# Both heads' attention scores multiplied back to back behind the tenth chunk, with a second probability buffer

## The reference

```python
scores = jnp.einsum('brhnqd,brhnkd->brhnqk', qb, kc) * (dh ** -0.5)
scores = jnp.where(mask, scores, -jnp.inf)
m = scores.max(-1, keepdims=True)
pr = jnp.exp(scores - m)
denom = pr.sum(-1, keepdims=True)
out = jnp.einsum('brhnqk,brhnkd->brhnqd', pr, vc) / denom
...
inner = jnp.einsum('bhqk,bhkv->bhqv', jnp.einsum('bhqd,bhkd->bhqk', qc, kc) * intra_decay, vc)
...
ret = head_group_norm(ret, ret_gn_g, ret_gn_b)
ret = (jax.nn.silu(ret_g.astype(jnp.float32)) * ret).astype(x.dtype)
merged = jax.nn.sigmoid(gate_a) * (attn @ w_attn_proj) + jax.nn.sigmoid(gate_r) * (ret @ w_ret_proj)
return merged @ w_out
```

## Time and profile before

| | |
|---|---|
| median of three runs | 1491.69 us (1491.23 to 1495.32) |
| the profiled execution | 1495.06 us, span 1493.3 us |
| TensorE busy with matmuls | 1460.3 us, 98% of the span |
| VectorE busy | 1047.4 us, 70% |
| ScalarE busy | 768.7 us, 51% |
| GpSimd busy | 45.9 us, 3% |
| mean granted TensorE clock | 0.993 |
| DMA | 292.00 MB, mean 196 GB/s |

### The profile page before, as it was taken

The page is one execution under the profiler, slowest core; times in us unless marked ns, Lnnn a source line. Parts: engine busy times, 40 slices in busy tenths (PEclk is TensorE's granted clock), DMA queues, the critical chain, the costliest instruction groups (busy, mean ns, idle before and its releaser), DMA issues.

```text
span 1493.3 us, 20079 instructions
## 1 busy us (share of the span) xinstructions
PE 1460.3 (98%) x8177; PEld 1278.8 (86%) x8177; DVE 1047.4 (70%) x1189; ACT 768.7 (51%) x813; POOL 45.9 (3%) x30
## 2 busy tenths in 40 slices
PE   9999999999999999999999999999999999999998
PEld 8888888888888888888888888888887888888886
DVE  5775675857665588777857667667567556887777
ACT  5545454454554456566544454545545444566562
POOL 0000000000000020000000000000000000200000
PEclk9999999999999999999999999999999999999999
DMA  9777596685856564655555956857748664665571
GB/s 309 237 189 207 172 212 202 182 214 169 224 178 224 179 219 166 211 197 198 178 174 170 226 182 176 218 182 198 211 159 208 201 222 162 220 205 189 172 239 39
DMA packets 357420, 292.00 MB, mean 196 GB/s; under 512 B 104544, under 2 KB 347744, under 8 KB 356704
## 3 DMA queue, kind: packets, MB, share of 16 engines
q1 hardware_dynamic: 356528, 290.14, 64.4%
q10 hardware_dynamic: 816, 0.79, 0.2%
HBM read 277.27 MB, written 13.63 MB: 195 GB/s over the span
## 4 chain that ended last, share of the span: by engine, by line
PE 80%; DVE 11%; ACT 3%; DMA 3%; SPq 1%; issue 1%; DVEq 0%; ACTq 0%
PE bank L1394 34%; PE bank L1399 17%; PE bank L1380 6%; PE bank L1381 6%; PE bank L1382 6%; DVE w_lo L819 5%; PE acc L1380 3%; PE acc L1381 3%; PE acc L1382 3%; ACT w_hi L462 2%; DMA raw<-w_in 1%; SPq L316 1%; PE acc L1529 1%; DVE scratch L1030 1%; DVE stat L1015 1%
## 5 line engine op out<-in xcount | busy, mean ns | idle before, releaser
L819 DVE TENSOR_TENSOR w_lo<-raw,w_hi 128x2048 fp32r<-128x2048 f32 x234 | 535.4, 2289 | 201.7 <-ACT w_hi L462 201.3
L1394 PE MATMUL bank<-xT_both,w_hi 128*128 128x512 f32 x2208 | 528.4, 392 | 2.2 <-DVE scratch L976 2.2
L462 ACT ACTIVATE w_hi<-raw 128x2048 fp32r<-128x2048 f32 x241 | 459.3, 1908 | 118.6 <-PE bank L1382 50.8
L1394 PEld LDWEIGHTS bank<-xT_both,w_hi 128*128 128x128 f32 x2208 | 407.7, 188 | 83.5 <-DVE scratch L976 2.8
L1399 PEld LDWEIGHTS bank<-xT_both,w_lo 128*128 128x128 f32 x2208 | 283.1, 191 | 10.7
L1399 PE MATMUL bank<-xT_both,w_lo 128*128 128x256 f32 x2208 | 286.5, 283 | 0.0
L1380 PE MATMUL bank<-w_hi,xT_both 128*128 128x512 f32 (+1 forms) x464 | 164.2, 354 | 16.3 <-DVE w_lo L819 15.9
L1381 PE MATMUL bank<-w_lo,xT_both 128*128 128x512 f32 (+1 forms) x464 | 163.2, 352 | 0.0
L1382 PE MATMUL bank<-w_hi,xT_both 128*128 128x512 f32 (+1 forms) x464 | 162.8, 351 | 0.0
L573 ACT ACTIVATE scratch<-bank 128x512 f32<-128x512 f32 x80 | 47.6, 595 | 212.0 <-PE bank L1399 212.0
L1380 PEld LDWEIGHTS bank<-w_hi,xT_both 128*128 128x128 f32 x464 | 89.7, 193 | 29.2 <-issue 17.8
(11 more groups left out here) (170 smaller groups left out, 1351.7 us busy)
## 6 DMA issues: line engine op xcount, KB each, us to landing
raw<-w_in SPq DMA_DIRECT2D x133, 1024.0 KB, 5.1
raw<-w_up SPq DMA_DIRECT2D x44, 1024.0 KB, 5.1
raw<-w_down SPq DMA_DIRECT2D x20, 1024.0 KB, 5.1
raw<-w_ret_proj SPq DMA_DIRECT2D x16, 1024.0 KB, 5.4
prob_blocks<-scratch SPq DMA_DIRECT2D x16, 512.0 KB, 4.3
scratch<-prob_blocks SPq DMA_DIRECT2D x64, 128.0 KB, 4.2
raw<-w_attn_proj SPq DMA_DIRECT2D x8, 1024.0 KB, 5.3
raw<-w_out SPq DMA_DIRECT2D x8, 1024.0 KB, 5.2
```

Of the source, the lines that this page charges most:

```text
L462: nc.scalar.activation(w_hi[:, s, :], raw[:, s, :], ACT.Copy).then_inc(hi_ready, 1)
L819: nc.vector.tensor_tensor(w_lo[:, s, :], raw[:, s, :], w_hi[:, s, :].bitcast(F32), ALU.subtract).then_inc(lo_ready, 1)
L1394: mm(pair[p][:, m, :], hi[:, o:o + P], src[:, k0 + k, :, :].rearrange("p a t -> p (a t)"), start=first and k == 0, stop=False)
```

## The change

There are two probability buffers and two sets of row statistics. The second buffer lies where the rotary step's temporaries are before and where `ret_t` is after. Behind chunk 9 TensorE multiplies the scores of both heads, head 1 into `acc[2]` and `acc[3]`. VectorE masks head 1 right after the rotary step of chunk 10, and at c = 11 takes its maximum and then normalises and turns both heads. ScalarE takes head 1's exponential at c = 11. Behind load 1' SyncE issues both `prob_out`, behind 2' both `prob_in`, and behind 4' only retention's blocks. The number of instructions is the same.

```diff
-        prob = view(2048, (TT, 512))
+        prob = [view(2048, (TT, 512)), view(6912, (TT, 512))]
...
                 if c == 1:
                     prob_out(0, it)
+                    prob_out(1, it)
                 if c == 2:
                     prob_in(0, it)
+                    prob_in(1, it)
                 if c == 4:
-                    prob_out(1, it)
                     ret_out(it)
-                    prob_in(1, it)
                     ret_in(it)
...
-                    if c == 14:
-                        exp(1)
...
+                    if c == 11:
+                        exp(1)
...
-                def mask_and_max(a):
+                def mask_scores(a):
                     if a == 0:
                         dve.wait_ge(const_in, 16)
+                    else:
+                        dve.wait_ge(roped_ready, it2 + 2)
                     dve.wait_ge(scores_done, it2 + a + 1)
                     for t in range(TT):
-                        ins = nc.vector.tensor_tensor(prob[:, t, :], acc[t][:, :], mask[:, t, :], ALU.add)
+                        ins = nc.vector.tensor_tensor(prob[a][:, t, :], acc[2 * a + t][:, :], mask[:, t, :], ALU.add)
                     ins.then_inc(scores_masked, 1)
+
+                def scores_max(a):
...
                 def turn_ret():
 
                     dve.wait_ge(ret_y_ready, it + 1)
+                    dve.wait_ge(prob_turned, it2 + 2)
...
                     if c == 14:
                         high_part(13, silu[:, 0:2, :], 1.0)
-                        mask_and_max(1)
                         group_stats()
...
                     if c == 10:
-                        mask_and_max(0)
+                        mask_scores(0)
+                        scores_max(0)
                         rotate(1)
+                        mask_scores(1)
                     if c == 11:
-                        normalise(0)
-                        turn_prob(0)
+                        scores_max(1)
+                        for a in range(2):
+                            normalise(a)
+                            turn_prob(a)
                     if c == 12:
                         decay_scores()
                     if c == 14:
-                        normalise(1)
-                        turn_prob(1)
                         dve.wait_ge(gn_rstd, it + 1)
...
                         scores(0)
+                        if it:
+                            pe.wait_ge(ret_y_ready, it)
+                        scores(1)
                     if c == 12:
                         pe.wait_ge(roped_ready, it2 + 2)
-                        if it:
-                            pe.wait_ge(ret_y_ready, it)
+                        pe.wait_ge(scores_masked, it2 + 2)
...
                     if c == 13:
-                        pe.wait_ge(scores_masked, it2 + 1)
-                        scores(1)
                         pe.wait_ge(decayed_lo_ready, it + 1)
```

More of the change, by code:

```diff
@@ L197, in program @@
         rs_ln = stat[:, 50:52]
[L198 to L201, removed]
+        neg_max = [stat[:, 52 + 26 * a:54 + 26 * a] for a in range(2)]
+        row_sum = [stat[:, 54 + 26 * a:56 + 26 * a] for a in range(2)]
+        row_inv = [stat[:, 56 + 26 * a:58 + 26 * a] for a in range(2)]
+        row_max = [stat[:, 58 + 26 * a:60 + 26 * a] for a in range(2)]
         half_neg = stat[:, 60:62]
@@ L520, in exp @@
                     for t in range(TT):
-                        ins = nc.scalar.activation(prob[:, t, :], prob[:, t, :], ACT.Exp, bias=neg_max[:, t:t + 1],
-                                                   accum_out=row_sum[:, t:t + 1])
+                        ins = nc.scalar.activation(prob[a][:, t, :], prob[a][:, t, :], ACT.Exp,
+                                                   bias=neg_max[a][:, t:t + 1], accum_out=row_sum[a][:, t:t + 1])
                     ins.then_inc(exp_done, 1)
@@ L1005, in rotate @@
                         dve.wait_ge(roped_ready, it2 + 1)
[L1007 removed]
+                def mask_scores(a):
                     if a == 0:
                         dve.wait_ge(const_in, 16)
+                    else:
+                        dve.wait_ge(roped_ready, it2 + 2)
                     dve.wait_ge(scores_done, it2 + a + 1)
                     for t in range(TT):
[L1012 removed]
+                        ins = nc.vector.tensor_tensor(prob[a][:, t, :], acc[2 * a + t][:, :], mask[:, t, :], ALU.add)
                     ins.then_inc(scores_masked, 1)
+                def scores_max(a):
                     dve.wait_ge(scores_masked, it2 + a + 1)
[L1015 removed]
+                    nc.vector.reduce_max(row_max[a], prob[a], AX.X).then_inc(row_max_ready, 1)
                     dve.wait_ge(row_max_ready, it2 + a + 1)
[L1017 removed]
+                    nc.vector.tensor_scalar(neg_max[a], row_max[a], -1.0, None, ALU.mult).then_inc(neg_max_ready, 1)
                 def normalise(a):
                     dve.wait_ge(exp_done, it2 + a + 1)
[L1021 removed]
+                    nc.vector.reciprocal(row_inv[a], row_sum[a]).then_inc(inv_ready, 1)
                     dve.wait_ge(inv_ready, it2 + a + 1)
                     for t in range(TT):
[L1024 removed]
+                        ins = nc.vector.tensor_scalar(prob[a][:, t, :], prob[a][:, t, :], row_inv[a][:, t:t + 1],
+                                                      None, ALU.mult)
                     ins.then_inc(prob_ready, 1)
@@ L1548, in scores @@
                     for t in range(TT):
-                        split_product(acc[t][:, 0:SEQ], near_hi[:, 0, a, t:SEQ:2], near_lo[:, 0, a, t:SEQ:2],
+                        split_product(acc[2 * a + t][:, 0:SEQ], near_hi[:, 0, a, t:SEQ:2], near_lo[:, 0, a, t:SEQ:2],
                                       near_hi[:, 1, a, :], near_lo[:, 1, a, :], True, True)
                         for i in range(1, NG):
-                            ins = mm(acc[t][:, (i + 1) * P:(i + 2) * P], qk[:, 2 * i, a, t:SEQ:2],
+                            ins = mm(acc[2 * a + t][:, (i + 1) * P:(i + 2) * P], qk[:, 2 * i, a, t:SEQ:2],
                                      qk[:, 2 * i + 1, a, t:SEQ:2], start=True, stop=True)
```

2 lines of the change are left out of this document (1 added, 1 removed).

## The result

The changed kernel takes 1480.2 us (median of four runs, 1479.87 to 1481.4), the kernel before in runs beside it 1493.51 us (1491.23 to 1495.57). The ratio is 0.9913, 95% interval 0.9893 to 0.9932. So it is faster by 0.9%, where 1468.2 us were forecast with a range from 1463.5 to 1479.0: the direction is right and the time lies outside the range. The profiled execution took 1479.87 us with a span of 1478.1 us, 15.2 us less than before.

The account below looks back on a forecast made before the run. TensorE was taken as the bound, busy for 1460.3 of 1493.3 us. The terms 13.8 + 1.1 + 3.5 + 8.5 = 26.9 us, taken from 1495.06, gave 1468.2 us, with a range of 1463.5 to 1479 us.

Parts of the forecast that it names:

- The six `w_lo` waits: TensorE's waits at chunk 1' of a turn: 0.35 of 2.65 us stay in each, 13.8 us gained.
- The cover at AV: Ahead of AV, `decayed_lo` would end 0.4 us before TensorE comes for it, in eight places; costed at nothing.
- The rival that ended slower than before: AV waits 3.1 us for `decayed_lo` and loses 1.7 us of clock, eight times: 1506 us; chance 0.05.
- GpSimd: VectorE waits 0.7 us for GpSimd's power before `ret_y`; as a rival, GpSimd becomes the bound: 1475 us, chance 0.11.
- The merge: Gate wait of 0.55 us goes in each layer, 1.1 us; `ret` wait falls 1.75 us in each layer, 3.5 us.
- The queue rival: Loads 3' and 4' under way in front of `ret_out` in the merge; `finish_ret` loses VectorE's gain: 1475 us, chance 0.06.
- The clock: All eight larger waits fall to 1.1 us or less; five clock drops of 1.7 us go: 8.5 us.
- the rule of the Trainium skill's page: Clock falls only when a wait outlasts the monitor's span, then in every pass; clock term 0, time 1476.6 us.

Follow-up runs that it names:

- Experiment 9: Changed kernel with the old queue order and head 1's maximum, exponential, normalise and turn back at c = 14; scores and mask stay early: 1501.11 us, ratio 1.0041.
- Experiment 10: Experiment 4 plus one unused maximum over 1024 elements on VectorE ahead of `to_lo` of chunk 14: 1473.94 us, ratio 0.9859.
- experiment 5: Changed kernel with `ret_out` held back on SyncE until VectorE is done with `to_lo` of chunk 2': 1477.86 us, ratio 0.9883.
- experiment 7: Changed kernel with `finish_ret` on ScalarE and VectorE behind the copies of chunk 2' instead of ahead of them: 1474.44 us, ratio 0.986.
- Experiment 4: Experiment 2 with `ret_out` and `ret_in` moved behind load 3', ahead of load 4': 1465.0 us, ratio 0.98.
- experiment 2: Changed kernel with `prob_in(1)` behind load 3' instead of behind load 2': 1484.33 us, ratio 0.9935.
- experiment 3: Experiment 2 with `ret_out` moved behind load 3', ahead of load 4'; `ret_in` stays behind load 4': 1470.04 us, ratio 0.9831.
- experiment 6: Kernel before with the queue edit alone: `prob_out(1)`, `ret_out`, `prob_in(1)` and `ret_in` behind load 3' instead of load 4': 1496.51 us, ratio 1.0003.
- experiment 8: Experiment 4 with the edit of experiment 7 on top: 1465.64 us, ratio 0.9803.
- experiment 1: Changed kernel with SyncE's issue order of the kernel before: `prob_out(1)`, `ret_out`, `prob_in(1)` and `ret_in` behind load 4': 1486.56 us, ratio 0.9943.

## Why the prediction was off, step by step

**The six `w_lo` waits: right.** 13.8 us were forecast, 14.7 came. VectorE's rows lie within 0.2 us of the working, in order: 275.82, 279.75, 283.81, 288.36, 291.67. Experiment 9 shows that the early maximum, exponential, normalise and turn carry it, not the scores on TensorE.

**The cover at AV: right.** 0.4 us were said to be in hand, and no wait for `mid_lo` at AV arose; in the changed kernel `decayed_lo` ended at 279.75 and AV started at 280.36, 0.6 us later. Experiment 10 shows how near it is. The rival that ended slower than before did not come about: the maximum was early enough, and ScalarE had the exponential done (272.9) before `to_hi` of chunk 14.

**GpSimd: right**, as a wait of 0.58 us that costs nothing more than was counted.

**The merge: this step failed.** "`turn_ret` ends 2.3 us earlier, and `ret_out`, `ret_in`, ... with it." The blocks were turned 2.4 us earlier, but `ret_in` started 1.0 us later than before and the blocks landed when they did before (`finish_ret` at 309.72 against 309.85; over the eight places 0.8 us earlier to 1.5 us later, 0.0 in the mean). I had bounded the queue's effect between "the whole rest of the wait gone" and "nothing gained at all", 3.5 us; the measured value lies beyond that bound (waits of 5.7 us, more than before). The bound itself was short: TensorE comes 0.55 us earlier in each layer, so with blocks no earlier the waits grow from 5.2 to 6.3 us. I took `ret_out`'s landing time from before as a constant, though it is a property of what stands ahead of it, and the change moved just that. It moved both sides: `ret_out` earlier, loads 3' and 4' later. The experiments in the tables, and the fifth by itself, show the cause: the load in front of `ret_out` is still under way.

**The queue rival had the place and not the price.** It gave 1475 us, for the merges alone. What it left out is that blocks come no sooner in the turns either, where TensorE is 2.45 us earlier and ScalarE stands at `finish_ret` in front of a copy that TensorE waits for: 3.2 us of idling in four places, and 1.0 us more in these turns that no row shows (experiment 7).

**The clock: right in kind.** The six waits fell to 0.2 us, and the drops behind them went; in the two merges waits and drops stayed, which the forecast had counted at 2 x 1.7 = 3.4 us. Here the rule of the Trainium skill's page (TensorE: Matmul & The Clock Gate, "HAM oscillation — how this bites in real kernels") would have forecast no gain from the clock; busy time fell by 4.2 us with the same matmuls, so the trace goes against it.

**The sum of the miss**, in the profiled execution: 1478.1 us of span against a forecast of 1495.06 - 26.9 - 1.76 = 1466.4 us, so 11.7 us. `ret` waits 5.7 - 1.7 = 4.0; L1082 3.2; two drops 2.8, at 1.4 each (busy time fell by 4.2 us for three; by the turns of the kernel before, 96.23 us without a drop and 97.83 to 97.85 with one, it is 1.6); two waits called "issue" at chunk 3' 0.5; short waits beyond their rows about 1.6 (an estimate: these six, at the 0.26 us that the four of experiment 7 have on average); L606 at a layer's start 0.8; less 0.9 for `w_lo` and 0.3 at the first wait of the program. That makes 11.7 us, and 12.1 with the drop at 1.6. Experiment 4, in which the queue's part is taken away, ran in 1465.0 us, 3.2 us under the forecast; the forecast had left 1.7 us of `ret` waits and 0.9 us too much for `w_lo`.

## What to carry to other kernels

When a change makes data ready earlier, work out what its transfer will now stand behind, in every queue: a transfer's time in a trace holds for what stands in front of it in that trace. A short transfer that someone waits for goes ahead of a large one that nobody needs yet; here that move brought 15 us, where the change had brought 13. And work that waits for a transfer passes the lateness on to whatever the code puts behind it on that engine, in every pass of the loop and not only where the wait was looked for.

## What the runs showed of the hardware

- A write of 512 KB to DRAM that was issued 0 to 1.7 us behind a 1 MB load on the same queue landed after 7.0 to 9.2 us (the changed kernel, experiments 2 and 7). Issued 3.0 to 10.8 us behind, it took 3.2 to 6.1 us (before, and experiments 3 to 6 and 8 to 10), and held back by 3 us it landed no later in the mean of the eight places (experiment 5).
- In the changed kernel and experiments 2, 5 and 7 the load was still under way in all 32 places, and the write landed 1.35 to 1.56 us behind it in 28 of them, 2.0 to 2.5 us in the last merge. In experiment 1, with another write of 512 KB between the two, it was 2.9 to 3.1 us.
- The granted clock behind a wait of TensorE, over the twelve traces between 50 and 1170 us: behind 112 waits of up to 1.65 us it was 1.00 over the next 5 us without exception. Behind 39 waits of 1.97 us and more it was lower (0.50 to 0.68) 29 times: behind all 17 waits for `ret`, 10 of 18 for `w_lo`, 2 of 4 at chunk 3'. So no rule of length alone decides between 2.0 and 3.0 us, and what else does was not tried.
- That equal waits are followed by a drop in one turn and not in another fits the spread of the runs: the kernel before ran in 1491.2 to 1498.9 us, that of experiment 4, with no such wait, in 1464.5 to 1465.8.
- Four waits of TensorE of 0.40 to 1.65 us by their rows cost 0.22 to 0.29 us more each than the row says (experiment 7). In experiment 10 two waits that grew by 0.85 us together lengthened a turn by 1.12 us.
